# Thirteen early expert tiles in three fp32r products, their low parts summed by an adding DMA, and a gate loop written out

## The chip, the core and the metric

The kernel runs on one core of one Trainium2 chip. The metric is the device time of one execution in microseconds (us), the median of three runs. A core has five engines that run their own instruction streams: TensorE (PE, matrix products; PEld is its weight load), VectorE (DVE), ScalarE (ACT), GpSimd (POOL) and SyncE (SP), which here only starts transfers. Engines meet at semaphores. SBUF is the on-chip memory of the operands, PSUM that of the products.

## The reference, cut to what matters

Two layers. Each has a mixing part (chunked attention, retention, a state space model), and behind it the part that this case is about, a product-key expert mixer on 256 tokens of width 1024:

```python
q = (hf @ w_q).reshape(t, PEER_HEADS, 2, PEER_QDIM // 2)
s = jnp.einsum('thsd,hskd->thsk', q, subkeys)
top_s, top_i = lax.top_k(s, PEER_TOPK)                      # 16 of 128 keys, twice
cand_s = top_s[:, :, 0, :, None] + top_s[:, :, 1, None, :]
cand_i = top_i[:, :, 0, :, None] * PEER_NKEYS + top_i[:, :, 1, None, :]
best_s, best_pos = lax.top_k(cand_s.reshape(...), PEER_TOPK)
expert = jnp.take_along_axis(cand_i.reshape(...), best_pos, axis=-1)
gate = jax.nn.softmax(best_s, axis=-1)
ub = jnp.take(u_tab, eb, axis=0)
vb = jnp.take(v_tab, eb, axis=0)
act = jax.nn.gelu(jnp.einsum('thkd,td->thk', ub, hb))
return jnp.einsum('thk,thkd->td', (gb * act), vb)
```

All inputs and the output are float32.

## The kernel before

The kernel doesn't gather experts. It takes the 16384 experts as 128 tiles of 128, computes every expert's score for every token, multiplies by a gate that is zero where the expert wasn't picked, and sums the value rows. A float32 product is made in one of two ways: directly in fp32 (8 products of 128x128 by 128x256 for a tile, which the profile shows as 16 records), or in three fp32r products: the operands are split into a rounded high part and the low rest, and high by high, high by low and low by high are added (24 products of that size).

A layer's expert part has these stages.

- **Top-16 stage.** Sixteen query steps `n`: PE multiplies a tile of `w_q` (`query`, lines 798 to 802, three fp32r products), ScalarE copies the result (line 1177) and PE forms two key score blocks (`key_scores`, line 783); VectorE finds the top 16 of them and, two steps behind, of the candidate sums (`top16`, lines 1360 to 1367; `pairs`, line 1605). ScalarE makes the high part of each `w_q` tile (`w_q_high`, line 1044), GpSimd the low part (line 988). The `w_q` tiles come through four ring slots (`stream`, line 432); a slot's next load waits for the low part of its last tile. Then VectorE turns positions into keys (lines 1629 to 1655) and writes picks (line 1658), which PE transposes (line 834) and ScalarE copies (line 1194).
- **Ahead tiles.** PE is not filled by this, so it computes the scores of 20 of the 128 expert tiles early: `A_TOP` = 11 in the top-16 stage (`ahead`, line 795, in fp32, from raw tiles RAWU and the fp32 activations H32), four of them inside query steps 5, 8, 11 and 14 (`AHEAD_AT`), six behind the last key scores, one between the two sides of the picks; and `A_GATE` = 9 in the gate stage (`ahead_step`, line 863). SyncE issues the eleven loads of 512 KB together, behind the fourth query tile (line 485). Their gelus (line 1172) are stored to DRAM and fetched back in the expert loop.
- **Gate stage.** 64 groups of four tokens, in eight turns of eight. VectorE makes one-hots of the picks (lines 1671, 1673 and 1677), GpSimd the key one-hots of groups 0, 3 and 6 of a turn (line 998) after a small copy (line 994), ScalarE scales the gates into those of groups 1, 3, 5 and 7, PE multiplies them (line 855), and ScalarE copies the product (line 1207). The one-hots lie in four banks, so group c waits for the product of group c-4. VectorE's first turn is written out, the other seven are a hardware loop; PE and ScalarE have all eight written out; GpSimd's turns 2 to 7 are a loop.
- **Expert loop.** The other `NM` = 108 tiles. For each PE forms scores (lines 884 and 886) and, one tile behind, adds the value product (line 893, 12 products of 512 columns); ScalarE and VectorE split `u` and `v` and do gelu and gate. In layer 0 tiles 26 to 81 also carry work for the next layer's modulation (line 1743), and from tile 82 (`AHEAD_TILE`) on VectorE gates one ahead tile beside each loop tile (`gate_ahead`).
- **Tail.** The value products of the 20 ahead tiles, from nine buffers RAWV.

Each engine runs its own list in the order of the text; there is no planner. SBUF is laid out by hand, at offsets in floats from one base, and buffers of one stage lie over those of another.

## Time and profile before

| | us |
|---|---|
| median of 3 runs | 2105.37 |
| lowest and highest | 2104.90, 2107.96 |
| the profiled execution | 2113.12 |
| its span | 2111.3 |
| mean granted TensorE clock | 0.988 of full |

The profile shows one execution, and it was some 8 us longer than the runs without a profiler. Its page gives the busy share of each engine, the span in 40 slices, the chain of work that ended last, and the costliest groups of instructions; the trace can be asked for a stretch of time, an engine or a line. A row of the chain or the timeline starts with its start and its length in us and ends with the count of instructions that it merges; brackets hold the idle time before it and what ended that. Busy shares say little here: the stages have different limits.

### The profile page before, as it was taken

What the parts mean: (1) busy time and instruction counts of PE and PEld (TensorE: products, weight loads), DVE (VectorE), ACT (ScalarE), POOL (GpSimd) and SP (SyncE); (2) the same over time, 40 slices, a digit from 0 to 9 for tenths busy, and PEclk for the clock granted to TensorE, in tenths of its full rate; (3) what the DMA queues carried; (4) which work ended last, traced back from release to release, by engine and by line L of the source; (5) the groups of instructions that cost most, each with busy time, mean ns of one, the idle gap of its engine ahead of it and who ended that gap; (6) DMA issues with size and microseconds to landing.
All of it is one profiled execution on the core that took longest, in us unless ns stands there. A gap on an engine that the chain in (4) does not pass through costs nothing.

```text
span 2111.3 us, 33992 instructions
## 1 busy us (share of the span) xinstructions
PE 2023.7 (96%) x11188; PEld 1741.2 (82%) x11188; DVE 1583.3 (75%) x3436; ACT 974.9 (46%) x1619; POOL 266.0 (13%) x309
## 2 busy tenths in 40 slices
PE   5999999999999999999999989889999999999998
PEld 4798989888888888888778989788888888888876
DVE  8884999767888888887657268886767676768854
ACT  3223248655544444444522242675555555554443
POOL 2003339200000000000010041780000000000000
PEclk9999999999999999999999999999999999999999
DMA  9466311355778877555453462114555555555562
GB/s 372 141 264 263 111 54 60 128 188 199 272 282 306 294 276 281 188 179 195 158 179 100 138 232 80 56 53 165 186 190 187 207 210 203 185 184 180 180 237 69
DMA packets 115739, 392.19 MB, mean 186 GB/s; under 512 B 12752, under 2 KB 20816, under 8 KB 115152
## 3 DMA queue, kind: packets, MB, share of 16 engines
q1 hardware_dynamic: 115664, 391.21, 52.0%
q8 instruction: 44, 0.72, 0.1%
q14 instruction: 31, 0.25, 0.0%
HBM read 384.35 MB, written 6.82 MB: 185 GB/s over the span
## 4 chain that ended last, share of the span: by engine, by line
PE 68%; DVE 21%; issue 5%; ACT 2%; DMA 2%; DVEq 1%; SPq 0%; POOL 0%
PE ps L893 25%; PE ps L884 13%; PE ps L886 6%; PE ps L627 5%; DVE v_lo L1698 4%; PE ps L855 3%; PE ps L640 3%; DVE next_w_ada_ring L1743 3%; PE ps L769 2%; DVE u_lo L1693 2%; DVE onehot_gate L1677 2%; DVE gated L1706 1%; ACT gelu L1246 1%; PE ps L795 1%; PE ps L800 1%
## 5 line engine op out<-in xcount | busy, mean ns | idle before, releaser
L884 PE MATMUL ps<-h_hi_lo,u_hi 128*128 128x512 f32 x1728 | 630.5, 399 | 6.2 <-DVE u_lo L1693 5.8
L886 PE MATMUL ps<-h_hi_lo,u_lo 128*128 128x256 f32 x1512 | 425.3, 281 | 0.0
L884 PEld LDWEIGHTS ps<-h_hi_lo,u_hi 128*128 128x128 f32 x1728 | 326.0, 189 | 76.8 <-issue 6.5
L886 PEld LDWEIGHTS ps<-h_hi_lo,u_lo 128*128 128x128 f32 x1512 | 286.9, 190 | 8.1
L893 PE MATMUL ps<-v_hi,gated_hi 128*128 128x512 f32 x864 | 272.0, 396 | 5.4 <-DVE gated_lo L1712 4.3
L1693 DVE TENSOR_TENSOR u_lo<-weight_ring,u_hi 128x1024 fp32r<-128x1024 f32 x216 | 263.6, 1221 | 14.3 <-ACT u_hi L1235 11.1
L893 PE MATMUL ps<-v_lo,gated_hi 128*128 128x512 f32 x864 | 268.2, 392 | 0.0
L893 PE MATMUL ps<-v_hi,gated_lo 128*128 128x512 f32 x864 | 266.3, 389 | 0.0
L1698 DVE TENSOR_TENSOR v_lo<-weight_ring,v_hi 128x1024 fp32r<-128x1024 f32 x216 | 263.3, 1219 | 0.5 <-ACT v_hi L1240 0.5
L1240 ACT ACTIVATE v_hi<-weight_ring 128x1024 fp32r<-128x1024 f32 x216 | 227.4, 1053 | 53.6 <-PE ps L893 53.5
L1246 ACT ACTIVATE gelu<-gelu 128x256 f32<-128x256 f32 x216 | 90.3, 418 | 329.2 <-DVE gelu L1702 329.2
L1235 ACT ACTIVATE u_hi<-weight_ring 128x1024 fp32r<-128x1024 f32 x216 | 227.5, 1054 | 11.9 <-DMA weight_ring<-in_u_tab_dram 11.3
L1706 DVE TENSOR_TENSOR gated<-gelu,gates_T 128x256 f32<-128x256 f32 x216 | 92.0, 426 | 133.7 <-ACT gelu L1246 133.7
L893 PEld LDWEIGHTS ps<-v_lo,gated_hi 128*128 128x128 f32 x864 | 162.2, 188 | 36.2
L893 PEld LDWEIGHTS ps<-v_hi,gated_lo 128*128 128x128 f32 x864 | 162.2, 188 | 36.0
L893 PEld LDWEIGHTS ps<-v_hi,gated_hi 128*128 128x128 f32 x864 | 157.0, 188 | 41.5 <-issue 14.1
L1244 ACT ACTIVATE gelu<-ps 128x256 f32<-128x256 f32 x216 | 81.6, 378 | 221.1 <-PE ps L884 221.0
L998 POOL TENSOR_SCALAR onehot_key<-iota,key_columns 128x128 f32<-128x128 f32 x192 | 158.2, 838 | 2.3 <-PE ps L855 2.3
L855 PEld LDWEIGHTS ps<-onehot_gate,onehot_key 128*128 128x128 f32 x1024 | 132.6, 191 | 29.4 <-DVE onehot_gate L1673 11.4
L855 PE MATMUL ps<-onehot_gate,onehot_key 128*128 128x128 f32 x1024 | 136.6, 276 | 15.8 <-DVE onehot_gate L1673 8.8
L1710 DVE CAST gated_hi<-gated 128x256 fp32r<-128x256 f32 x216 | 63.5, 294 | 105.3 <-PE ps L893 100.2
L988 POOL TENSOR_TENSOR w_q_lo<-weight_ring,w_q_hi 128x1024 fp32r<-128x1024 f32 x32 | 76.0, 2381 | 335.7 <-ACT w_q_hi L1044 335.7
(314 smaller groups left out, 3115.4 us busy)
## 6 DMA issues: line engine op xcount, KB each, us to landing
weight_ring<-in_u_tab_dram SPq DMA_DIRECT2D x224, 512.0 KB, 4.5
weight_ring<-in_v_tab_dram SPq DMA_DIRECT2D x216, 512.0 KB, 3.5
next_w_ada_ring<-in_w_ada_dram SPq DMA_DIRECT2D x56, 512.0 KB, 4.4
weight_ring<-in_w_in_dram SPq DMA_DIRECT2D x46, 512.0 KB, 3.7
w_ada_ring<-in_w_ada_dram SPq DMA_DIRECT2D x40, 512.0 KB, 8.7
v_tail<-in_v_tab_dram SPq DMA_DIRECT2D x40, 512.0 KB, 4.7
weight_ring<-in_w_q_dram SPq DMA_DIRECT2D x32, 512.0 KB, 3.6
u_ahead<-in_u_tab_dram SPq DMA_DIRECT2D x22, 512.0 KB, 9.1
```

Source lines behind the costliest of these rows:

```text
L627: last = mm(PS[:, bank, 0:T], w[:, k, :], HT[:, k, :], start=(k == 0), stop=(k == KT - 1))
L855: last = mm(PS[:, c % 4, q * P:(q + 1) * P], OHB[:, c % 4, q, :], OHA[:, c % 4, q, :], start=True, stop=True)
L884: last = mm(both, UH[:, b, k, :], HB[:, :, k, :], start=(k == 0), stop=(k == KT - 1))
L886: mm(PS[:, 4 + b, 0:T], UL[:, b, k, :], HH[:, k, :], start=False, stop=False)
L893: last = mm(PS[:, 2 * t + d, :], g[:, t * P:(t + 1) * P], v[:, b, d * 512:(d + 1) * 512], start=start and n == 0, stop=stop and n == 2)
L998: last = nc.gpsimd.tensor_scalar(OHB[:, POOL_GROUPS[b] % 4, q, :], IOTA[:, 0:P], KEY4[:, b, q:q + 1], None, ALU.is_equal)
L1235: return fn(UH[:, b, :, :], RING[:, slot, :].rearrange("p (k n) -> p k n", n=P), ACT.Copy).then_inc(u_hi, 1)
L1240: return fn(VH[:, b, :], RING[:, slot, :], ACT.Copy).then_inc(v_hi, 1)
L1246: return fn(GE[:, b, :], GE[:, b, :], ACT.Gelu_apprx_tanh).then_inc(gelu_done, 1)
L1693: v.tensor_tensor(UL[:, b, :, :], RING[:, b, :].rearrange("p (k n) -> p k n", n=P), UH[:, b, :, :].bitcast(F32), ALU.subtract).then_inc(u_ ...
L1698: v.tensor_tensor(VL[:, b, :], RING[:, 2 + b, :], VH[:, b, :].bitcast(F32), ALU.subtract).then_inc(v_split, 1)
L1706: v.tensor_tensor(G32[:, :], GE[:, b, :], WT[:, i, :], ALU.mult).then_inc(g_prod, 1)
```

## The change

`A_TOP` goes from 11 to 13, so 22 tiles are ahead and 106 remain in the loop. The thirteen tiles are multiplied in three fp32r products. ScalarE writes the high part of a raw tile and its negated copy (`cut_ahead`); then a DMA issued by GpSimd reads the tile once more from DRAM and adds it into the negated copy, given to the DMA as a float32r tile; what stands there is the low part. Raw tiles have a ring of three buffers, high and low parts a ring of six pairs. Eight cuts stand in query steps (`CUT_AT`), five behind. The fp32 activations H32, still needed in the gate stage, are made later. The negated copy is written as float32r as well. The tail's nine buffers move to the start of the region. VectorE's loop over turns 1 to 7 of the gate stage becomes a Python loop, so its instructions are written out.

```diff
-A_TOP = 11
-A_RING = 11
+A_TOP = 13
+A_RING = 3
+CUT_AT = (1, 3, 5, 7, 9, 10, 12, 15)
-        V_AT = (0, 1024, 2048, 3072, 4096, 20480, 21504, 22528, 23552)
+        V_AT = range(0, 1024 * TAIL_RING, 1024)
+        AHEAD_PLACE = (0, 1, 2, 3, 0, 1, 2, 3, 4, 5, 0, 1, 2)
@@ SyncE
+                def ahead_raw(a):
+                    if a >= A_RING:
+                        sp.wait_ge(ahead_cut, l * A_TOP + a - A_RING + 1)
+                    sp.dma_start(RAWU[a % A_RING][:, :, :], u_tab[l, NM + a].rearrange("p (k n) -> p k n", n=P)).then_inc(
+                        in_ahead[a % A_RING], 16)
-                        for a in range(A_TOP):
-                            sp.dma_start(RAWU[a][:, :, :], u_tab[l, NM + a].rearrange("p (k n) -> p k n", n=P)).then_inc(in_ahead[a // 2], 16)
+                        for a in range(A_RING):
+                            ahead_raw(a)
+                    for a in range(A_RING, A_TOP):
+                        if a - A_RING < 7 and n == TILE_Q + min(15, CUT_AT[a - A_RING] + 4):
+                            ahead_raw(a)
+                ahead_raw(10)
@@ behind the first expert loads
                 ahead_late(1)
+                for a in range(11, A_TOP):
+                    ahead_raw(a)
@@ TensorE, ahead(a)
+                    pe.wait_ge(*ahead_summed(l, a))
                     for k in range(KT):
-                        last = mm(PS[:, 2 + a % 2, 0:T], RAWU[a][:, k, :], H32[:, k, :], start=(k == 0), stop=(k == KT - 1))
+                        mm(out, hi[:, k, :], HH[:, k, :], start=(k == 0), stop=False)
+                        mm(out, hi[:, k, :], HL[:, k, :], start=False, stop=False)
+                        last = mm(out, lo[:, k, :], HH[:, k, :], start=False, stop=(k == KT - 1))
@@ GpSimd
+                def add_raw(a):
+                    pool.wait_ge(ahead_cut, l * A_TOP + a + 1)
+                    place = AHEAD_PLACE[a]
+                    gp.dma_start(UAL[place][:, :, :], u_tab[l, NM + a].rearrange("p (k n) -> p k n", n=P),
+                                 accum_op=ALU.add).then_inc(ahead_low[place], 16)
+                    if n - 3 in CUT_AT:
+                        add_raw(CUT_AT.index(n - 3))
+                for a in range(7, A_TOP):
+                    add_raw(a)
@@ ScalarE
+                def cut_ahead(a):
+                    place = AHEAD_PLACE[a]
+                    act.wait_ge(*ahead_loaded(l, a))
+                    if place >= 4:
+                        act.wait_ge(q_mm, l * 16 + 20 - place)
+                    elif a >= 4:
+                        before = max(b for b in range(a) if AHEAD_PLACE[b] == place)
+                        act.wait_ge(ahead_mm, l * AHEAD + before + 1)
+                    fn(UAH[place][:, :, :], RAWU[a % A_RING][:, :, :], ACT.Copy)
+                    fn(UAL[place][:, :, :], RAWU[a % A_RING][:, :, :], ACT.Copy, scale=-1.0).then_inc(ahead_cut, 1)
+                    if n in CUT_AT:
+                        cut_ahead(CUT_AT.index(n))
-                gelu_ahead(4)
-                gelu_ahead(5)
+                for a in range(4, 9):
+                    gelu_ahead(a)
+                    cut_ahead(a + 4)
@@ VectorE, gate stage
-                with dve.Fori(1, 8) as i:
+                for i in range(1, 8):
                     for c in range(8):
                         dve.wait_ge(w_mm, i * 8 + (l * 64 + c - 3))
                         onehots(c, i * 32 + 4 * c)
@@ VectorE, expert loop
-                expert_tiles(AHEAD_TILE + AHEAD, NM - 2)
+                if AHEAD_TILE + AHEAD < NM - 2:
+                    expert_tiles(AHEAD_TILE + AHEAD, NM - 2)
```

## Rows read from the trace of the kernel before

**Rows 1.** The page: busy time by engine, and the chain by engine

```profile
PE 2023.7 (96%) x11188; PEld 1741.2 (82%) x11188; DVE 1583.3 (75%) x3436; ACT 974.9 (46%) x1619; POOL 266.0 (13%) x309
PE 68%; DVE 21%; issue 5%; ACT 2%; DMA 2%; DVEq 1%; SPq 0%; POOL 0%
```

**Rows 2.** The chain in order of time (start, us, what): value products, both layers

```profile
860.01 2.97 PE ps L893 x12
...
975.81 2.93 PE ps L893 x12
...
1001.96 58.43 PE ps L893 x252
...
1885.41 2.74 PE ps L893 x12
1890.96 2.75 PE ps L893 x12
2011.73 3.01 PE ps L893 x12
...
2037.96 57.88 PE ps L893 x252
```

**Rows 3.** The same chain, query steps of layer 1

```profile
1269.66 0.45 PE ps L783 x4
...
1272.98 0.45 PE ps L783 x4
...
1276.74 3.46 PE ps L795 x16
```

**Rows 4.** Groups by line, then timelines, chain and window, of the query steps

```profile
L800 PE MATMUL ps<-h_hi_lo,w_q_hi 128*128 128x256 f32 x128 | 39.1, 305 | 2.5 <-DVE h_hi_lo L1594 1.8 <-POOL w_q_lo L988 0.7
...
L1044 ACT ACTIVATE w_q_hi<-weight_ring 128x1024 fp32r<-128x1024 f32 x14 | 14.7, 1048 | 3.0 <-DMA weight_ring<-in_w_q_dram 3.0
...
L783 PE MATMUL ps<-subkeys_T,query_T 128*128 128x128 f32 x64 | 10.6, 290 | 3.3 <-DVE key_scores L1367 2.9 <-ACT query_T L1177 0.3
...
203.50 9.44 POOL L988 TENSOR_TENSOR w_q_lo<-weight_ring,w_q_hi 128x1024 fp32r<-128x1024 f32 x4 [2.74 <-ACT w_q_hi L1044]
...
204.02 8.94 DVE L1605 TENSOR_TENSOR candidates<-top_scores 128x32 f32<-128x32 f32 x4
...
216.43 4.51 PE ps L795 x16
...
1240.17 0.71 PE L783 MATMUL ps<-subkeys_T,query_T 128*128 128x128 f32 x4 [1.29 <-ACT query_T L1177]
1241.54 0.39 PE L800 MATMUL ps<-h_hi_lo,w_q_hi 128*128 128x256 f32 x1 [0.66 <-POOL w_q_lo L988]
...
1237.00:1247.00 10.00, 8.05 (x53) 7.66 (x52) 7.76 (x45) 6.69 (x13) 7.05 (x3) 0.83 0.58 215
```

**Rows 5.** The end of layer 0's top-16 stage: the chain, and PE's timeline

```profile
264.61 0.24 DVE best L1360
...
294.31 0.63 PE ps L834 x8
...
265.08 20.89 PE L795 MATMUL ps<-h_fp,u_ahead 128*128 128x256 f32 x96
```

**Rows 6.** Gate stage: windows (PE, PEld, DVE, ACT, POOL, clock, DMA), then timelines

```profile
311.20:322.39 11.19, 10.84 (x81) 10.10 (x81) 10.40 (x26) 9.45 (x26) 10.25 (x16) 1.00 0.18 59
...
1344.55:1357.11 12.56, 11.08 (x81) 10.03 (x81) 10.24 (x25) 9.48 (x26) 11.17 (x16) 1.00 0.15 52
...
1353.20 3.80 POOL L998 TENSOR_SCALAR onehot_key<-iota,key_columns 128x128 f32<-128x128 f32 x4
...
1357.15 2.54 POOL L998 TENSOR_SCALAR onehot_key<-iota,key_columns 128x128 f32<-128x128 f32 x4
...
1357.11 1.13 PE L855 MATMUL ps<-onehot_gate,onehot_key 128*128 128x128 f32 x8 [1.26 <-DVE onehot_gate L1673]
```

**Rows 7.** DMA issues of the page: KB each, median us from issue to landing

```profile
u_ahead<-in_u_tab_dram SPq DMA_DIRECT2D x22, 512.0 KB, 9.1
u_ahead_even<-in_u_tab_dram SPq DMA_DIRECT2D x10, 512.0 KB, 3.4
```

More of the change, by code:

```diff
@@ L183, in trunk @@
         CBN = at("next_cond", 4096, [P, D])
-        RAWU = [at(f"u_ahead_{a}", 2560 if a == 10 else 19200 + 1024 * a, [P, KT, P]) for a in range(A_TOP)]
+        RAWU = [at(f"u_ahead_{i}", o, [P, KT, P]) for i, o in enumerate((27392, 28416, 2560))]
+        UAH = [at(f"u_ahead_hi_{i}", o, [P, KT, P], F32R) for i, o in enumerate((19200, 21248, 23296, 25344, 38912, 40960))]
+        UAL = [at(f"u_ahead_lo_{i}", o, [P, KT, P], F32R) for i, o in enumerate((20224, 22272, 24320, 26368, 41984, 44032))]
         GEA = at("gelu_ahead", 29440, [P, A_TOP, T])
@@ L191, in trunk @@
         GER = at("gelu_back", 5120, [P, AHEAD, T])
[L192 to L194 removed]
+        GHA = at("gated_ahead_hi", 10752, [P, AHEAD, T], F32R)
+        GLA = at("gated_ahead_lo", 16384, [P, AHEAD, T], F32R)
+        V_AT = range(0, 1024 * TAIL_RING, 1024)
         RAWV = [at(f"v_tail_{a}", o, [P, D]) for a, o in enumerate(V_AT)]
@@ L339, in trunk @@
         s_sum = sem("expert_scores_summed")
-        in_ahead = [sem(f"u_ahead_pair_loaded_{a}") for a in range((A_RING + 1) // 2)]
+        in_ahead = [sem(f"u_ahead_loaded_{a}") for a in range(A_RING)]
+        ahead_cut = sem("u_ahead_hi_and_negated_done")
+        ahead_low = [sem(f"u_ahead_low_summed_{i}") for i in range(6)]
         in_late = [sem(f"u_ahead_late_loaded_{i}") for i in range(2)]
@@ L375, in trunk, with ahead_summed @@
         LATE_STORES = [len(range(i, A_GATE, 4)) for i in range(4)]
+        AHEAD_PLACE = (0, 1, 2, 3, 0, 1, 2, 3, 4, 5, 0, 1, 2)
         def ahead_loaded(l, a):
-            pair = a % A_RING // 2
-            tiles = [b // A_RING for b in range(A_TOP) if b % A_RING // 2 == pair]
-            return in_ahead[pair], 16 * (l * len(tiles) + sum(b <= a // A_RING for b in tiles))
+            return in_ahead[a % A_RING], 16 * (l * len(range(a % A_RING, A_TOP, A_RING)) + a // A_RING + 1)
+        def ahead_summed(l, a):
+            place = AHEAD_PLACE[a]
+            return ahead_low[place], 16 * (l * AHEAD_PLACE.count(place) + AHEAD_PLACE[:a + 1].count(place))
         TILE_IN, TILE_OUT, TILE_Q = 0, IN_TILES, IN_TILES + KT
@@ L788, in ahead @@
                 def ahead(a):
-                    pe.wait_ge(*ahead_loaded(l, a))
-                    if a == 0:
-                        pe.wait_ge(h32_done, l + 1)
+                    pe.wait_ge(*ahead_summed(l, a))
                     if a >= 2:
                         pe.wait_ge(ahead_gelu, l * AHEAD + a - 1)
+                    hi, lo, out = UAH[AHEAD_PLACE[a]], UAL[AHEAD_PLACE[a]], PS[:, 2 + a % 2, 0:T]
                     for k in range(KT):
-                        last = mm(PS[:, 2 + a % 2, 0:T], RAWU[a][:, k, :], H32[:, k, :], start=(k == 0), stop=(k == KT - 1))
+                        mm(out, hi[:, k, :], HH[:, k, :], start=(k == 0), stop=False)
+                        mm(out, hi[:, k, :], HL[:, k, :], start=False, stop=False)
+                        last = mm(out, lo[:, k, :], HH[:, k, :], start=False, stop=(k == KT - 1))
                     last.then_inc(ahead_mm, 1)
@@ L865, in ahead_step @@
                         last.then_inc(ahead_mm, 1)
+                pe.wait_ge(h32_done, l + 1)
                 for k in range(KT):
@@ L1169, in _ @@
                 w_q_high(l, 2)
+                def cut_ahead(a):
+                    place = AHEAD_PLACE[a]
+                    act.wait_ge(*ahead_loaded(l, a))
[6 more added lines that the diff above has]
+                    fn(UAL[place][:, :, :], RAWU[a % A_RING][:, :, :], ACT.Copy, scale=-1.0).then_inc(ahead_cut, 1)
                 def gelu_ahead(a):
@@ L1179, in _ @@
                         w_q_high(l, n + 3)
-                    if n < 4:
-                        for k in (2 * n, 2 * n + 1):
-                            last = fn(H32[:, k, :], HT[:, k, :], ACT.Identity, bias=MODS[l][:, SH2, k:k + 1])
-                        if n == 3:
-                            last.then_inc(h32_done, 1)
+                    if n in CUT_AT:
+                        cut_ahead(CUT_AT.index(n))
                     if n in AHEAD_AT:
                         gelu_ahead(AHEAD_AT.index(n))
-                gelu_ahead(4)
-                gelu_ahead(5)
+                for a in range(4, 9):
+                    gelu_ahead(a)
+                    cut_ahead(a + 4)
                 act.wait_ge(gate_in, l + 1)
                 fn(GATE[:, :, :], GATE[:, :, :], ACT.Exp).then_inc(gate_exp, 1)
-                for a in range(6, A_TOP):
+                for a in range(9, A_TOP):
                     gelu_ahead(a)
+                    if a < 11:
+                        for k in range(4 * (a - 9), 4 * (a - 9) + 4):
+                            last = fn(H32[:, k, :], HT[:, k, :], ACT.Identity, bias=MODS[l][:, SH2, k:k + 1])
+                        if a == 10:
+                            last.then_inc(h32_done, 1)
                 act.wait_ge(pickt_mm, l + 1)
```

2 lines of the change are left out of this document (removed).

## The prediction

> **What bounds the kernel now.** I read the page first: TensorE (PE) is busy 96% of the span and is 68% of the chain that ended last, VectorE (DVE) 21% [rows 1]. So PE's own work is the price of a tile, except where the chain leaves PE. The chain in order of time shows where. In the expert loop one tile costs 5.55 us on PE (start to start of the value products), 5.8 us where VectorE also gates the ahead tiles, and a tile of the tail only its value products: 58.43 us and 57.88 us for 21 of them [rows 2]. In the top-16 stage the query steps follow each other by 3.32 us, and an ahead tile adds 3.46 us [rows 3]: PE again, with a few holes that come from a late weight tile [rows 4]. From the last key scores (264.6 us in layer 0) to the gate products VectorE's chain of picks sets the time, some 29.7 us in which PE has room [rows 5]. In the gate stage a turn of eight groups takes 11.19 us in layer 0 and 12.56 us in layer 1, though the instructions are the same [rows 6].
>
> **Part 1, two tiles leave the loop.** There are 13+9 ahead tiles instead of 11+9, so the loop runs over 106 tiles, not 108. Gating of ahead tiles begins at tile 82 as before, and now covers 22 tiles: 82 to 103, with 2 plain tiles behind them instead of 6. Per layer 4 plain tiles go (4 x 5.55 = 22.2 us) and 2 gating tiles come (2 x 5.79 = 11.6 us in layer 0 by the step from 860.01 to 975.81 over 20 tiles; in layer 1, 120.77 us over 21 tiles, 5.75 each, 11.5 us): -10.6 and -10.7 us. The tail gets 2 tiles: 58.43/21 = 2.78 and 57.88/21 = 2.76 us each, +5.6 and +5.5 us. Net -5.0 and -5.2, together **-10.2 us**. Cover that shrinks: the tail's value tiles are fetched after the last ahead tile is gated, which was some seven tiles before the loop's end and is now two to three. From there PE still has about two score groups (2.8 us) and three value groups (2.75 us), some 14 us, and the same tiles land in 3.5 to 4.7 us [rows 7]: nothing, and a few us if four at once took over 10.
>
> **Part 2, the form of the ahead product.** Today 8 fp32 products (16 records) take 3.46 us. The query's form, 24 fp32r products of the same size, takes 3.32 - 0.45 = 2.87 us [rows 3]. Four ahead tiles stand inside the query steps, where PE is the chain: 4 x 0.59 = 2.36 us per layer, **-4.7 us**. Is VectorE late next? Its step there is 3.86 us, PE's would be (16 x 3.32 + 4 x 2.87)/16 = 4.04: it just keeps pace.
>
> **Part 3, the loads ahead of the query weights.** Eleven ahead loads are issued in one go before the fifth query tile, and ScalarE waits for that tile, 3.0 us in layer 0. PE waits behind it 0.3 + 0.7 us in layer 0 and 1.29 + 0.66 us in layer 1. Then in layer 0 GpSimd makes up four low parts without a pause (9.44 us), four tiny sums of VectorE take 8.94 us beside it, and PE waits 2.9 us for VectorE; the ahead tile after that wait takes 4.51 instead of 3.46 us. In layer 1 the granted clock from 1237 to 1247 us is 0.83, that is 1.2 GHz for 3.4 of 10 us, after PE's waits: 1.7 us lost [rows 4]. With 3 loads in front of it the tile comes some 10 us sooner and none of this need happen: -(1.0 + 2.9 + 1.05) = -4.95 and -(1.95 + 1.7) = -3.65, **-8.6 us**.
>
> The new waits: SyncE now waits for a cut at ScalarE before a reload, with the next query load queued behind it. A cut ends some 3.5 us into its step (query copy 0.38, query high part 1.05, two copies 2.1), and two transfers end 5 us later: 8.5 us. The tile is wanted by PE 4 x 3.32 = 13.3 us into the step, less 3.4 us for its high and low parts: 1.4 us spare, and 2.9 more where an ahead tile lies between, as it does for each of them. ScalarE waits up to 1.5 us there; query copies have 2.9 us of room. Nothing.
>
> **Part 4, the end of the top-16 stage.** Counted from the last key scores, PE today ends six ahead tiles at +21.2 us, and the first side's picks follow from there [rows 5]. Eight at 2.87 us end at +23.0. Then side 0 (2.1), the gates (0.4), the last ahead tile (2.9) and three quarters of side 1 (1.5) give +29.9, where VectorE has its last picks at +29.7; ScalarE's changed order (two table loads around the exponential, 1.28 us each, before the gelu of tile 9) costs 0.1. I put **+0.4 us per layer, +0.8**.
>
> **Part 5, the adding DMA.** The chain for tile a+4 is: tile a ends, gelu 0.4, two copies 2.1, adding DMA Z, product. PE comes round in 4 x 2.87 = 11.5 us, so Z may be 11.5 - 2.87 - 2.5 = 6.1 us. No row shows an adding DMA or any from GpSimd. Ends: 3.9 us, as a plain tile with its issue (3.4 to 3.6 landing, 0.43 issue), and 13 us or more if it queues as the eleven did (9.1 landing) and its extra read of the destination adds 3.5 [rows 7]. Nearest is the plain tile, with twice the traffic in SBUF: 7.5 us with issue. The ring of six then stalls PE by 1.4 us once in tiles 8 to 11, and tile 12 (start at 10.8 + 2Z = 25.8) not more. **+1.5 per layer, +3.0** (0 to 11 each). Inside the query steps tile 0 has about 8.7 us from its cut: covered. GpSimd's issues also hold VectorE's small sums, as in rows 4: 0 to 2.9 us per layer, I take 1: **+2.0**.
> The Trainium skill's page SBUF — State Buffer (SBUF: two separate sides) says that a DMA issued by GpSimd has its descriptors kept waiting while VectorE runs an operation on both ports. It speaks against this part; by it Z would be longest in VectorE's long arithmetic between +10 and +29. No row here has such a DMA. The page DMA: Bandwidth & Descriptors (Anatomy of one DMA — SWDGE path) gives 2.0 us plus bytes/436 GB/s, 3.2 us for a tile; an estimate by that would make the +3.0 zero.
>
> **Part 6, the gate loop written out.** The loop's turn costs VectorE gaps of 0.1 to 0.15 us. But VectorE then waits 0.68 us (layer 0) or 1.77 us (layer 1) for PE, and PE's first group of a turn starts 0.1 us after GpSimd's four key one-hots: 1353.20 + 3.80 = 1357.00, and PE at 1357.11. (The row puts the wait to VectorE, whose one-hots had ended by 1356.62; GpSimd ends last.) The same holds in layer 0, where PE starts 0.11 us after GpSimd too. So the turn is a ring of PE (3.97 us), GpSimd's copy and one-hots for the seventh group, and those for the next first; VectorE enters by slowing GpSimd: four one-hots cost 2.54 us with it idle, 3.25 to 3.33 in layer 0, 3.81 to 3.88 in layer 1 [rows 6]. Written out, the loop saves no time by its branch. It shifts VectorE by a tenth of a us against GpSimd, and the two layers part by no more than that. Bounds per turn: PE's own 8 x 1.325 = 10.6 us, and 12.56; seven turns a layer: from -(0.6 + 1.96) x 7 = -17.9 to +1.37 x 7 = +9.6 us. I take **0**.
> The Trainium skill's page Runtime: NRT & Kernel Launch (Instruction fetch mechanics) says that a taken branch breaks the sequential prefetch and can stall an engine. By it the unrolling would return at most the visible gaps, 0.24 x 14 = 3.4 us; the rows show them inside VectorE's waiting, so the sum takes none.
>
> **Sum**: -10.2 - 4.7 - 8.6 + 0.8 + 3.0 + 2.0 + 0 = **-17.7 us**. The profiled execution took 2113.1 us (span 2111.3), so it would take 2095.4; the median of the runs, 2105.4, is 7.7 below it and moves alike: **2087.7, say 2088 us**.
>
> **The rivals.**
> A, forecast: gate turns stay about as they are. 2088 (2081 to 2095). Chance 0.40.
> B, the gate turns get shorter: layer 1 falls into layer 0's pattern (-9.6 us: 2078) or both become bound by PE (2070). For it: same instructions, two speeds. Against: PE waits for GpSimd, not for the loop. 0.25.
> C, layer 0 falls into the 12.56 us pattern: +9.6, 2097. For it: VectorE without gaps takes the lead over GpSimd more often. 0.13. The same SBUF page's rule, one of the two engines holds the shared port for a whole instruction, is behind both B and C; the one-hots at 2.54 against 3.88 us agree that they hinder each other, though both run on in part.
> D, the added tiles come late: Z = 10 us. Tile 12 starts at 10.8 + 20 = 30.8 instead of 25.8; 5 us a layer in place of 1.9: 2094, with stalls inside the query steps 2100. 0.14.
> E, slower than before: the adding DMA itself becomes the bound. Each layer then pays 2Z - 15; with all other terms kept the gain of 17.7 + 3.8 = 21.5 us is gone at 10.8 us a layer, Z = 12.9 us. At Z = 15 the time is 2084 + 30 = 2114. For it: 9.1 us landings under load. 0.08.
>
> **How the numbers follow.** Below 2101.2 (0.2%, about what a measurement of this kernel can tell from no change) lie A, B, C and most of D: 0.87. Within 0.2%: the rest of D and a mild E, 0.06. Slower: 0.07. For 8 in 10 I leave out the far end of B and E: 2072 to 2101.
>
> **What would show it.** Right: the score rows of the loop fall from 216 to 212 tiles and the two tails take 63.9 and 63.4 us; ScalarE's wait for query weights nearly vanishes; ahead groups take 2.9 us; the turn of the gate stage, 11.2 and 12.6 us; GpSimd's one-hots tell which pattern. Wrong: adding DMAs landing over 9 us, PE waiting in front of ahead tiles 8 to 12, small sums of VectorE over 1 us each, or a tail whose high parts wait for their load.

## The result, and the profile after

The changed kernel takes 2116.5 us (median), 1.006 times the kernel before, 95% interval 1.0045 to 1.0074: 11 us slower by the medians and 13 by the ratio, where 17.7 us less were forecast. Three later executions, one each of e4 (3366 us), e11 (2199 us) and e12 (3215 us), fell into a slower state of the chip and are left out of all medians and ratios. Its profiled execution took 2121.41 us (span 2119.6). The page of the kernel after (busy time and the chain, as [rows 1]; the queues, whose columns are packets, MB and share of the 16 DMA engines' span; DMA issues, as [rows 7]):

```profile
PE 2018.2 (95%) x11396; PEld 1747.8 (82%) x11396; DVE 1575.3 (74%) x3428; ACT 1016.2 (48%) x1663; POOL 285.9 (13%) x335
q1 hardware_dynamic: 115952, 392.26, 52.5%
q0 software_dynamic: 3744, 13.63, 3.4%
PE 67%; DVE 18%; DMA 6%; issue 4%; ACT 3%; POOL 1%; DVEq 1%; SPq 0%; ACTq 0%
weight_ring<-in_w_q_dram SPq DMA_DIRECT2D x32, 512.0 KB, 5.7
u_ahead<-in_u_tab_dram SPq DMA_DIRECT2D x26, 512.0 KB, 4.5
u_ahead_lo<-in_u_tab_dram POOLq DMA_DIRECT2D x26, 512.0 KB, 9.1
```

TensorE's share of the chain hardly moved, VectorE's fell from 21% to 18%, and DMA, 2% of it before, is 6% now; the last line, the adding DMAs' landing, is new. The chain in order of time names the places in layer 0's top-16 stage:

```profile
269.86 17.63 DMA u_ahead<-in_u_tab_dram
287.54 0.94 issue
288.48 1.05 ACT u_ahead_lo L1216
```

The plain load of ahead tile 11 takes 17.6 us. ScalarE's and VectorE's timelines beside it (start, us, engine, line, operation; in brackets the idle time before it and what ended it):

```profile
279.72 0.38 ACT L1220 ACTIVATE gelu_ahead<-ps 128x256 f32<-128x256 f32 x1 [4.13 <-PE ps L818]
287.51 1.06 ACT L1215 ACTIVATE u_ahead_hi<-u_ahead 128x1024 fp32r<-128x1024 f32 x1 [7.41 <-DMA u_ahead<-in_u_tab_dram]
...
292.99 0.42 ACT L1236 ACTIVATE gates<-gates 128x256 f32<-128x256 f32 x1
```

```profile
281.68 5.45 DVE L1709 SCALAR_TENSOR_TENSOR picked_keys<-pos_a_f,top_keys_f 128x256 bf16<-128x256 f32 x16
293.43 0.42 DVE L1703 TENSOR_REDUCE gate_sum<-gates 128x16 f32<-128x256 f32 x1 [6.30 <-ACT gates L1236]
...
306.19 0.94 DVE L1728 TENSOR_SCALAR onehot_gate<-iota,picks_T 128x128 f32<-128x128 f32 x3 [6.15 <-ACT picks_T L1245]
```

ScalarE stands 7.4 us for tile 11; the gates' exponential is queued behind its parts; VectorE waits 6.3 us for that and 6.2 us for the transposed picks. In [rows 5] VectorE's chain of picks ran through, but for 1.6 us before the first one-hot made from the transposed picks. Windows of the two parts of layer 0's top-16 stage, from the first h_T to VectorE's positions ("past") and from there to the first one-hot; of before, then of after (busy us of PE, PEld, DVE, ACT, POOL, then granted clock, DMA share, GB/s):

```profile
186.92:275.63 88.71, 82.96 (x561) 78.81 (x562) 80.66 (x469) 31.60 (x56) 33.30 (x14) 0.94 0.44 158
275.63:295.81 20.18, 19.04 (x135) 16.58 (x135) 18.11 (x54) 3.91 (x7) 0.00 (x0) 1.00 0.18 72
```

```profile
190.17:275.03 84.86, 77.08 (x616) 76.11 (x616) 75.42 (x469) 47.03 (x68) 42.00 (x24) 0.96 0.71 198
275.03:306.19 31.16, 25.96 (x215) 25.20 (x216) 18.19 (x54) 13.51 (x23) 2.59 (x3) 0.89 0.76 216
```

The first part gave back 3.9 us; the second costs 11.0 us more for the same 18.1 us of VectorE, with the DMA engines' share at 0.76 instead of 0.18. In layer 1 the parts are 87.8 and 33.9 us (before: 86.3 and 20.2). In all seventeen traces the second part is 18.6 to 18.7 us plus VectorE's two waits, for the exponential and for the transposed picks: 6.3 + 6.2 us in layer 0 of after, 5.9 + 9.2 in layer 1, 0 + 1.6 in both layers before. The loop and the tails did what was forecast: 276 value products in one go, 63.89 us in layer 0.

### The profile page after: what moved, and what is told of

It reads as the page before. It is cut to its first block, busy times and chain, and to the rows that moved or that the text cites. A ratio compares the mean times of both kernels' runs of the same rounds, so it can differ in the third digit from the quotient of the medians.

```text
span 2119.6 us, 33931 instructions
## 1 busy us (share of the span) xinstructions
PE 2018.2 (95%) x11396; PEld 1747.8 (82%) x11396; DVE 1575.3 (74%) x3428; ACT 1016.2 (48%) x1663; POOL 285.9 (13%) x335
## 3 DMA queue, kind: packets, MB, share of 16 engines
q1 hardware_dynamic: 115952, 392.26, 52.5%
## 4 chain that ended last, share of the span: by engine, by line
PE 67%; DVE 18%; DMA 6%; issue 4%; ACT 3%; POOL 1%; DVEq 1%; SPq 0%; ACTq 0%
PE ps L918 25%; PE ps L909 12%; PE ps L911 6%; PE ps L649 5%; PE ps L879 4%; DVE v_lo L1749 4%; PE ps L662 3%; DMA weight_ring<-in_w_q_dram 3%; PE ps L791 3%; DVE next_w_ada_ring L1794 3%; DVE u_lo L1744 2%; PE ps L887 2%; DMA u_ahead<-in_u_tab_dram 2%; DVE gated L1757 1%; ACT gelu L1297 1%
## 5 line engine op out<-in xcount | busy, mean ns | idle before, releaser
L909 PE MATMUL ps<-h_hi_lo,u_hi 128*128 128x512 f32 x1696 | 617.6, 398 | 6.2 <-DVE u_lo L1744 5.8
L911 PE MATMUL ps<-h_hi_lo,u_lo 128*128 128x256 f32 x1484 | 417.5, 281 | 0.0
L909 PEld LDWEIGHTS ps<-h_hi_lo,u_hi 128*128 128x128 f32 x1696 | 319.6, 189 | 74.9 <-issue 6.5
L911 PEld LDWEIGHTS ps<-h_hi_lo,u_lo 128*128 128x128 f32 x1484 | 281.3, 190 | 8.0
L918 PE MATMUL ps<-v_hi,gated_hi 128*128 128x512 f32 x848 | 267.6, 397 | 5.1 <-DVE gated_lo L1763 3.9
L1744 DVE TENSOR_TENSOR u_lo<-weight_ring,u_hi 128x1024 fp32r<-128x1024 f32 x212 | 258.7, 1221 | 14.6 <-ACT u_hi L1286 11.3
L918 PE MATMUL ps<-v_lo,gated_hi 128*128 128x512 f32 x848 | 263.5, 392 | 0.0
L918 PE MATMUL ps<-v_hi,gated_lo 128*128 128x512 f32 x848 | 261.7, 390 | 0.0
L1749 DVE TENSOR_TENSOR v_lo<-weight_ring,v_hi 128x1024 fp32r<-128x1024 f32 x212 | 258.3, 1218 | 0.0
L1297 ACT ACTIVATE gelu<-gelu 128x256 f32<-128x256 f32 x212 | 88.6, 418 | 333.7 <-DVE gelu L1753 333.7
L1291 ACT ACTIVATE v_hi<-weight_ring 128x1024 fp32r<-128x1024 f32 x212 | 223.1, 1053 | 51.1 <-PE ps L918 51.1
L879 PEld LDWEIGHTS ps<-onehot_gate,onehot_key 128*128 128x128 f32 x1024 | 133.1, 192 | 23.6 <-DVE onehot_gate L1724 9.1
```

Source lines behind the costliest of these rows:

```text
L879: last = mm(PS[:, c % 4, q * P:(q + 1) * P], OHB[:, c % 4, q, :], OHA[:, c % 4, q, :], start=True, stop=True)
L909: last = mm(both, UH[:, b, k, :], HB[:, :, k, :], start=(k == 0), stop=(k == KT - 1))
L911: mm(PS[:, 4 + b, 0:T], UL[:, b, k, :], HH[:, k, :], start=False, stop=False)
L918: last = mm(PS[:, 2 * t + d, :], g[:, t * P:(t + 1) * P], v[:, b, d * 512:(d + 1) * 512], start=start and n == 0, stop=stop and n == 2)
L1291: return fn(VH[:, b, :], RING[:, slot, :], ACT.Copy).then_inc(v_hi, 1)
L1297: return fn(GE[:, b, :], GE[:, b, :], ACT.Gelu_apprx_tanh).then_inc(gelu_done, 1)
```

## The experiments

All kernels in one table. The ratio goes against the kernel before on the same chip (whose median moved between 2103.7 and 2108.2 us from one set of runs to the next, so small differences are read from ratios). The last columns are, for each layer, h_T to positions + positions to first one-hot, from the starts of those instructions in each trace.

| kernel | us | ratio, 95% | layer 0 | layer 1 |
|---|---|---|---|---|
| before | 2105.4 | 1 | 88.7 + 20.2 | 86.3 + 20.2 |
| b_again (before, one execution) | 2108.2 | | 90.6 + 20.2 | 86.3 + 21.5 |
| after | 2116.5 | 1.006 (1.0045-1.0074) | 84.9 + 31.2 | 87.8 + 33.9 |
| e1_unroll_alone | 2108.1 | 1.001 (0.9997-1.0024) | 88.6 + 20.2 | 88.6 + 20.2 |
| e2_loop_back | 2115.9 | 1.0043 (1.0027-1.006) | 86.9 + 31.5 | 87.8 + 31.1 |
| e3_raws_first | 2110.2 | 1.0018 (1.0008-1.0027) | 88.6 + 26.8 | 87.6 + 26.2 |
| e4_query_first | 2115.3 | 1.0044 (1.0028-1.0059) | 85.2 + 30.8 | 87.9 + 30.0 |
| e5_both_orders | 2107.7 | 1.0012 (0.9997-1.0026) | 85.1 + 28.3 | 87.8 + 24.3 |
| e6_early_cuts | 2103.3 | 0.9988 (0.9975-1.0002) | 85.5 + 25.3 | 86.8 + 23.1 |
| e7_plain_second | 2095.2 | 0.9952 (0.9934-0.9969) | 82.6 + 22.7 | 83.9 + 24.8 |
| e8_no_adding | 2085.5 | 0.9906 (0.988-0.9933) | 82.7 + 20.2 | 81.4 + 20.2 |
| e9_subtract | 2138.1 | 1.0145 (1.0122-1.0169) | 108.1 + 20.3 | 105.4 + 20.2 |
| e10_none_at_end | 2098.3 | 0.9959 (0.9944-0.9974) | 85.1 + 20.6 | 86.2 + 20.6 |
| e11_mixed | 2111.3 | 1.0032 (1.0019-1.0044) | 94.6 + 20.3 | 93.7 + 20.9 |
| e12_half_added | 2091.5 | 0.9939 (0.9917-0.9961) | 80.7 + 24.3 | 81.2 + 25.9 |
| e13_fp32_at_end | 2092.4 | 0.9929 (0.9913-0.9945) | 82.1 + 23.6 | 83.4 + 22.1 |
| e14_all_fp32 | 2097.7 | 0.995 (0.9936-0.9963) | 84.4 + 23.8 | 84.4 + 23.8 |

The last two columns come from one execution each, and they scatter: before and b_again are the same kernel and differ by 1.9 us to the positions of layer 0 and 1.4 us at the end of layer 1; after and e2 run the same instructions up to layer 0's one-hots and differ by 2.1 us to its positions, and, with no difference but the gate loop, by 2.8 us at the end of layer 1. So a difference of 2 to 3 us in one of these columns shows little by itself.

**The gate loop.** Before with `for i in range(1, 8)`, after with `dve.Fori(1, 8)`, and before once more for its trace:

> The kernel before with VectorE's gate loop written out and nothing else. Theory (the loop's turn, not the new top-16 stage, took 7.2 us out of layer 1's gate stage, 112.8 to 105.6 us): 2098 us, ratio 0.9966, layer 1's gate stage near 106 us, layer 0's still near 104. Rival (layer 1's gate stage changed because of something else in the new kernel, as the start of its one-hots against GpSimd): 2105 us, layer 1 still at 112 to 113 us.

> The changed kernel with VectorE's gate loop as a loop again. Theory: layer 1's gate stage goes back from 105.6 to about 112.8 us, layer 0's stays near 104: 2116.5 + 7 = 2123.5 us. Rival (the writing out did nothing, the shorter stage comes from elsewhere): 2116.5 us, layer 1 at 106 us.

> The kernel before, once more, for its trace. Theory (the 9 us of layer 1's gate stage, 110.4 against 101.3 us in layer 0, are how that one execution fell, since neither writing the loop out nor looping it again in the changed kernel showed them): layer 1's gate stage at 101 to 104 us and a span near 2103 us. Rival (they belong to the kernel with the loop and the old top-16 stage): 110 us again in layer 1.

The theory fell. Written out alone, the loop brings nothing (0 to 0.2% slower); put back, it costs nothing (2115.9 against 2116.5). The stage (first one-hot to VectorE's first sum of the expert loop) takes 101.3 and 110.4 us in the profiled execution of before, but 99.7 and 100.9 in b_again, 101.5 and 101.6 in e1, 101.2 and 101.1 in e2. The slow turns of [rows 6] were how that one execution fell. They account for its 2113.1 us against a median of 2105.4, and for this: the profiled executions understate what the change costs: 8 us between them, 13 by the ratio.

**The order on SyncE's queue.** For tile 11, and for the query weights:

```
-                ahead_raw(10)
+                for a in range(10, A_TOP):
+                    ahead_raw(a)
                 for v in (0, 1):
...
                 ahead_late(1)
-                for a in range(11, A_TOP):
-                    ahead_raw(a)
```

> The changed kernel with the plain loads of ahead tiles 11 and 12 issued right after that of tile 10, ahead of the three expert loads and the first late load. Theory (tile 11's load takes 17.6 us because four other tiles stand in front of it, and ScalarE, then the gates' exponential and VectorE's picks wait behind it): ScalarE's wait for the plain tile falls from 7.4 and 8.1 us to 0 to 2 us, VectorE's for the exponential from 6 us to under 2, and each layer's top-16 stage is 5 to 7 us shorter: 2105 us. Rival (the adding DMAs of tiles 8 to 12 are what is slow, the loads in front are no matter): tile 11's product is late by its adding DMA anyway, 0 to 2 us a layer, 2113 to 2116 us.

```
-                        if a - A_RING < 7 and n == TILE_Q + min(15, CUT_AT[a - A_RING] + 4):
+                        if a - A_RING < 7 and n == TILE_Q + min(15, CUT_AT[a - A_RING] + 6):
```

> The changed kernel with each plain reload inside the query steps issued two query loads later (4 becomes 6 in the offset from the cut's step), so that SyncE waits for the cut only when the query loads of the next two steps are out. Theory (order on SyncE's queue: the query load stands behind SyncE's wait for a cut): ScalarE's waits for query weights fall from 19.0 us in layer 0's stage and from 38.2 us in layer 1 to near before's 3 us, and the two stages get some 12 us shorter together: 2104 us. Rival (bandwidth: adding DMAs slow every query load in flight, whatever the order): landings of query loads stay at 5 to 6 us, waits fall by less than half, 2112 to 2116 us.

> The changed kernel with both re-orderings of SyncE's queue (plain tiles 11 and 12 ahead of the expert loads; plain reloads two query loads later). Theory after the first runs (VectorE is the bound from the first scores to its picks, so the missing query weights cost only what VectorE waits; the end of the stage costs by tile 11's late load): the gains add, 6 us from the first and 1 to 3 from the second: 2108 to 2110 us, from the stage's start to the positions about 85 us, from there to the one-hots 26 to 27 us. Rival (the two compete for the same DMA engines: an earlier reload makes the adding DMAs late): no better than the first alone, 2110 to 2112 us.

The first holds in its mechanism: ScalarE's wait for the plain tile falls from 7.4 to 0.8 us, VectorE's for the exponential is gone, and the end of the stage is 4.3 and 7.6 us shorter. It brings about half of what was expected, 2110.2 us instead of 2105. What is left at the end of layer 0 (26.8 us against 20.2) is this wait (engine, tile, line, releaser: us in total, times, longest):

```profile
DVE onehot_gate L1727 <- ACT picks_T L1244: 8.2, 1, 8.2
```

It was 1.6 us before. TensorE makes these picks behind the late ahead tiles. The second experiment shows where I had misread the stage. ScalarE's wait for query weights in layer 0 of after (19.0 us; 18.5 in layer 1, where my expectation had put 38.2):

```profile
ACT w_q_hi L1080 <- DMA weight_ring<-in_w_q_dram: 19.0, 8, 5.9
```

In e4 it vanishes from ScalarE's list in both layers, yet the positions come after 85.2 and 87.9 us, as in after: 2115.3. 19 us of ScalarE's waiting there cost nearly nothing.

What does count is VectorE. Its time to the positions is, in all seventeen traces, a constant of 59.2 to 59.6 us, plus its waits for scores, plus its 64 small sums of candidates:

| kernel, layer | to positions | small sums | waits for scores | rest |
|---|---|---|---|---|
| before, 0 | 88.7 | 22.3 | 5.7 + 1.2 | 59.5 |
| after, 1 | 87.8 | 15.6 | 4.6 + 8.3 | 59.3 |
| e4, 0 | 85.2 | 20.9 | 4.5 + 0.4 | 59.4 |
| e8, 0 | 82.7 | 17.4 | 5.7 | 59.6 |
| e14, 0 | 84.4 | 19.2 | 5.8 | 59.4 |
| e9, 0 | 108.1 | 42.8 | 5.7 | 59.6 |

VectorE's waits in that window of layer 1 of after (engine, tile, line, releaser: us in total, times, longest):

```profile
DVE best L1411 <- PE ps L805: 8.3, 6, 2.5
DVE top_scores L1411 <- PE ps L805: 4.6, 2, 3.7
```

e4 trades one for the other: in layer 1 the waits fall by 7.2 us and the sums grow from 15.6 to 22.7. The traces show where the sums grow: in all seventeen, a sum that lies beside none of GpSimd's subtractions takes at most 0.20 us. In layer 1 of after 13 of the 64 sums lie beside a subtraction and take 8.4 us, in e4 it is 15 sums and 15.7 us. That VectorE's waiting is what moves the sums away from the subtractions is likely, and was not tested by itself.

e5 has both orders and takes 2107.7 us, close to its theory (2108 to 2110); the intervals of e3 and e5 overlap.

**The adding DMA itself.** First, on top of e5, ScalarE's parts for tiles 8 to 12 one ahead tile earlier:

```
+                cut_ahead(8)
                 for a in range(4, 9):
                     gelu_ahead(a)
-                    cut_ahead(a + 4)
+                    if a < 8:
+                        cut_ahead(a + 5)
```

> As the kernel with both re-orderings, and ScalarE makes the high and negated parts of tiles 8 to 12 one ahead tile earlier (tile 8's before the gelu of tile 4, tile 9's before that of tile 5, and so on). Theory (what is left of the end of the stage, 26.5 us against before's 20.2, is mostly TensorE waiting for adding DMAs that take 8 to 12 us where 6.1 fit): one ahead tile more of slack, 2.9 us, takes most of the 4.2 us of waits, and the end of the stage is 23 to 24 us: 2 to 3 us less a layer, 2103 to 2105 us. Rival (the adding DMAs share bandwidth: issued earlier they land as late): end of the stage stays at 26 us, 2108 us.

Then, each by itself in the changed kernel: a plain copy instead of the addition, no second load, none for tiles 7 to 12, and the addition for half of each tile.

```
-                    gp.dma_start(UAL[place][:, :, :], u_tab[l, NM + a].rearrange("p (k n) -> p k n", n=P),
-                                 accum_op=ALU.add).then_inc(ahead_low[place], 16)
+                    gp.dma_start(UAL[place][:, :, :], u_tab[l, NM + a].rearrange("p (k n) -> p k n", n=P)
+                                 ).then_inc(ahead_low[place], 16)
```

> The changed kernel with GpSimd's second load as a plain copy, without the addition; the low parts are then the whole tiles, so the ahead tiles of the output are computed from other weights. Theory (adding itself is dear: it reads and writes the destination): landings fall from 9.1 to about 5 us and TensorE's waits for them vanish, the rest of the queueing stays; 2112 us. Rival (the length comes from 512 KB more beside the other loads and from GpSimd's queue, not from the addition): landings stay over 8 us and the time at 2116 us.

```
-                    pe.wait_ge(*ahead_summed(l, a))
+                    pe.wait_ge(ahead_cut, l * A_TOP + a + 1)
...
-                    if n - 3 in CUT_AT:
-                        add_raw(CUT_AT.index(n - 3))
-                for a in range(7, A_TOP):
-                    add_raw(a)
```

> The changed kernel without the 26 adding DMAs; TensorE waits for the cut alone. It leaves the addition out, so low parts are minus the high parts. Theory (second loads crowd the DMA engines and hold up plain tile 11, and GpSimd's issues and TensorE's waits come on top): query loads land in under 4.5 us, tile 11's plain load in under 10, TensorE's and ScalarE's waits at the end of the stage nearly vanish, end of the stage 22 us: 2116.5 - 2 x 9 = 2098 us. Rival (the end of the stage is long because of the order on SyncE's queue and of ScalarE's exponential behind the last cuts, with or without the additions): 2108 us or more.

For e10 only the additions of tiles 7 to 12 go (the last two of these lines), and TensorE waits for the cut alone from tile 7 on.

> The changed kernel without the adding DMAs of tiles 7 to 12 (TensorE waits for their cut alone; their low parts are minus the high parts), those of tiles 0 to 6 kept. Theory from the stage times (the additions cost 11 to 13.6 us a layer after the query steps and 2.2 to 6.3 us in them): the end of the stage falls to 20 to 22 us, the time from the start to the positions stays at 85 to 88 us: 2116.5 - 2 x 11 = 2094 us. Rival (what the seven inside the query steps delay is carried through the end): 2100 us or more.

```
-                    gp.dma_start(UAL[place][:, :, :], u_tab[l, NM + a].rearrange("p (k n) -> p k n", n=P),
+                    gp.dma_start(UAL[place][:, 0:KT // 2, :], u_tab[l, NM + a].rearrange("p (k n) -> p k n", n=P)[:, 0:KT // 2, :],
                                  accum_op=ALU.add).then_inc(ahead_low[place], 16)
```

> The changed kernel with adding DMAs over the first half of each tile only, 256 KB in place of 512; it leaves the addition out for the other half. Theory (what costs is the time of the shared DMA engines: 3.4% of 16 engines' span for 26 adding DMAs, 2.8 us each, against 1.8%, 1.4 us each, as plain copies): the cost of 31 us over the kernel without them is about halved, landings fall from 9.1 to 5 or 6 us, 2099 to 2102 us. Rival (what costs is fixed per DMA, GpSimd's issue, the descriptors and the latency, whatever the size): landings stay over 8 us, 2110 us or more.

Without the second load the kernel takes 2085.5 us: **the additions cost 31 us** (32 by the ratios). As plain copies they cost 9.7, over half a tile 5.9 (10 and 7 by the ratios; e8's own interval is 5.6 us wide to either side, so these two are not told apart, but both are far from 31). The queue's line of the page, of e7 and then of e12:

```profile
q0 software_dynamic: 3744, 13.63, 1.8%
```

```profile
q0 software_dynamic: 3744, 6.82, 1.9%
```

In us of all 16 engines for one of the 26: 3.4% of 2119.6 / 26 = 2.8 us with the addition, 1.8% of 2094.1 / 26 = 1.45 us as a copy, 1.9% of 2089.7 / 26 = 1.5 us for an added half. A plain load by SyncE takes 52.5% of 2119.6 / 392.26 MB x 0.524 MB = 1.5 us. So adding doubles the engines' time, and the price follows that time, though not in proportion: none 0, half 6 to 10, all of it 31 us. The instructions that issue the second loads, with shortest, median and longest ns of the issue, and under each the time from issue to landing; of after, e7 and e12:

```profile
L1013 POOL DMA_DIRECT2D u_ahead_lo<-in_u_tab_dram x26: 849/862/1017, 206.3 to 1331.2; - x26
DMA to landing us min/median/max: 5.6/9.1/12.4
```

```profile
L1013 POOL DMA_DIRECT2D u_ahead_lo<-in_u_tab_dram x26: 530/570/743, 202.7 to 1308.7; - x26
DMA to landing us min/median/max: 4.5/6.7/10.3
```

```profile
L1013 POOL DMA_DIRECT2D u_ahead_lo<-in_u_tab_dram x26: 847/864/1022, 201.3 to 1303.0; - x26
DMA to landing us min/median/max: 4.1/7.5/9.1
```

e12 issues as slowly as after and moves as many packets, and it costs 6 us: the issue on GpSimd and the number of packets are not the price. Latency alone does not order the kernels either: e12's loads land later than e7's in the median and it is no slower. Both the engines' time and the landing are worse in after, and the two were not varied apart. My theory for e8 (2098) was 12 us too high, that for e7 (2112) took too little for the addition, and that for e12 (half the price, 2099 to 2102) too much for the half. The two windows of layer 0 in e8, to set against those of after:

```profile
189.40:272.10 82.70, 79.94 (x646) 79.61 (x647) 75.86 (x469) 48.36 (x70) 33.56 (x14) 0.95 0.48 179
272.10:292.28 20.18, 19.24 (x188) 18.54 (x187) 18.11 (x54) 12.41 (x21) 0.00 (x0) 1.00 0.24 98
```

The DMA share is 0.48 and 0.24 instead of 0.71 and 0.76, and the end of the stage is 20.2 us again. What the addition does to others shows in the landings (shortest, median, longest us, of the plain ahead loads of after, then of e8):

```profile
DMA to landing us min/median/max: 3.6/4.5/17.6
```

```profile
DMA to landing us min/median/max: 3.4/3.7/6.1
```

Tile 11's load stands behind the same four tiles in e8 and needs at most 6.1 us (and no plain ahead load of e7 more than 9.0). The order on SyncE's queue was thus only the place where the additions struck. e10 takes 18.2 of the 31 us off (21 by the ratios), between its theory (2094) and its rival (2100 or more): the end of the stage is 20.6 us in both layers, and the time to the positions stays. The seven additions a layer in the query steps carry the rest. In the traces of after and e8 the difference lies in VectorE's waits: for scores 2.7 and 8.4 us more in after (layers 0 and 1), for the exponential 6.3 and 5.9, for the transposed picks 4.6 and 7.7. Its sums are 0.3 and 1.8 us shorter. e6's cuts save 4.4 us, as expected: with more slack, some of the additions' time is hidden, and TensorE still waits 4.1 us in four times in layer 0.

**Another way to the low part.** GpSimd subtracts, as for the query weights; then only for tiles 7 to 12 (both with the orders and cuts of e6):

```
-                    gp.dma_start(UAL[place][:, :, :], u_tab[l, NM + a]..., accum_op=ALU.add).then_inc(ahead_low[place], 16)
+                    gp.tensor_tensor(UAL[place][:, :, :], RAWU[a % A_RING][:, :, :],
+                                     UAH[place][:, :, :].bitcast(F32), ALU.subtract).then_inc(ahead_low[0], 1)
```

> The kernel with both re-orderings and the earlier cuts, and GpSimd makes the low parts by subtraction from the tile that is already in SBUF (as it does for the query weights, 2.35 us each) in place of the 26 adding DMAs; ScalarE's negated copies go, a plain reload waits for the subtraction. Theory (what the change loses is the second, adding load of each tile: 31 us between the changed kernel and the one without it): end of the stage back to 20 to 21 us; VectorE's small sums run longer beside 13 more subtractions, 2 to 4 us a layer: 2090 to 2094 us, some 12 us under before. Rival (GpSimd's arithmetic holds VectorE, which is the bound of the stage, as much as the DMAs did): to the positions 88 to 90 us instead of 82.7, 2100 us or more.

> The kernel with both re-orderings and the earlier cuts, with adding DMAs for tiles 0 to 6 and GpSimd's subtraction for tiles 7 to 12, most of which fall behind the query steps. Theory (adding DMAs are dear at the end of the stage, 14 us in two layers by the kernel without them there; subtractions are dear only beside VectorE's small sums of the query steps, 1.8 us each there by the kernel that subtracts everywhere): to the positions 85 to 88 us, end of the stage 20 to 22 us, 2096 to 2099 us, some 8 us under before. Rival (VectorE's last picks and positions up to +10 us after the last scores are held as the small sums are): two to four us more a layer, 2101 to 2106 us.

Both theories fell, the first badly: 2138.1 us. Groups of VectorE to the positions in layer 0, of e9 and then of e8 (busy us, mean ns of one):

```profile
L1656 DVE TENSOR_TENSOR candidates<-top_scores 128x16 f32<-128x16 f32 x32 | 19.7, 656 | 0.0
L1656 DVE TENSOR_TENSOR candidates<-top_scores 128x32 f32<-128x32 f32 x16 | 14.0, 877 | 0.5
L1656 DVE TENSOR_TENSOR candidates<-top_scores 128x8 f32<-128x8 f32 x16 | 9.1, 569 | 0.0
```

```profile
L1652 DVE TENSOR_TENSOR candidates<-top_scores 128x32 f32<-128x32 f32 x16 | 8.7, 542 | 0.5
L1652 DVE TENSOR_TENSOR candidates<-top_scores 128x8 f32<-128x8 f32 x16 | 4.7, 296 | 0.0
L1652 DVE TENSOR_TENSOR candidates<-top_scores 128x16 f32<-128x16 f32 x32 | 4.0, 165 | 0.0
```

Thirteen subtractions more make the sums 25.4 us longer, 2.0 us for each of 2.4 us. The end of the stage is 20.3 us, so the ahead tiles no longer delay it. In e11 the six subtractions begin at 262.5 us, when VectorE still sorts the last scores, and its sums take 28.8 us where they take 20.9 in e6: 94.6 us to the positions. The Trainium skill's page SBUF — State Buffer (SBUF: two separate sides) has the two engines share one pair of ports, held for a whole instruction where VectorE reads two operands from SBUF and GpSimd reads SBUF too. The sums here agree (2.0 us for each subtraction of 2.4), and at this place that rule was worth more than anything in my sum.

**A version that beats both.** Tiles 0 to 6 keep three products and their addition; 7 to 12 are plain fp32 products from the loaded tile, as before. Then (e14) all thirteen so, in eleven buffers, with tiles 11 and 12 loaded into the first two again:

```
+                        if a >= 7:
+                            last = mm(out, ahead_at(a)[:, k, :], H32[:, k, :], start=(k == 0), stop=(k == KT - 1))
+                            continue
                         mm(out, hi[:, k, :], HH[:, k, :], start=(k == 0), stop=False)
...
-                for a in range(7, A_TOP):
-                    add_raw(a)
```

> Thirteen ahead tiles with the orders of the kernel with both re-orderings, where tiles 0 to 6 keep the three products and their adding DMA, and tiles 7 to 12 are plain fp32 products from the loaded tile as in the kernel before: no cut, no second load, and the fp32 copy of the hidden state made in the first query steps again. Theory (additions are dear where several stand in a row behind the last scores, 14 us in two layers; fp32 products cost 0.6 us more each, of which TensorE has some to spare before the picks): the end of the stage 22 to 23 us instead of 31, to the positions 86 us, 2099 to 2102 us, under before's 2105 by 0.2 to 0.3%. Rival (six products of 3.46 us put TensorE in front of the picks: 3 x 2.9 + 6 x 3.5 + 3.6 = 33 us from the last scores where VectorE needs 29.7): end of the stage 24 us or more, 2104 us.

```
-                        if a >= 7:
+                        if a >= 0:
...
-                    elif a >= A_RING:
-                        sp.wait_ge(ahead_cut, l * 7 + a - A_RING + 1)
+                    if a >= 11:
+                        sp.wait_ge(ahead_mm, l * AHEAD + a - 10)
...
+                        if a < 11 and n == TILE_Q + a + 1:
+                            ahead_raw(a)
```

> Thirteen ahead tiles, all as plain fp32 products in the form of the kernel before: eleven buffers, tile 11 and 12 loaded again into the first two, no cut, no adding DMA; three loads ahead of the fifth query tile and the others one for each query step. Theory (VectorE bounds the stage up to its picks, so TensorE's 0.6 us less a tile is worth nothing inside the query steps, and the three products with their second loads are pure cost): as fast as the kernel with fp32 products at the end, 2090 to 2094 us. Rival (the cheaper form does carry part of the gain in the query steps, as the prediction had it, 4.7 us in four tiles of two layers): 2096 to 2100 us.

e13 takes 2092.4 us, 0.7% under before and 1.3% under the changed kernel, and is better than its theory: to the positions 82.1 and 83.4 us. e14 goes to the rival: 2097.7 us. Both have the two tiles fewer in the loop and the spread loads. What parts them is the cheaper form of tiles 0 to 6 together with its seven additions a layer, and the steps at which the plain loads are issued. It is worth 0.2% or 4.4 us by the ratios, whose intervals overlap a little: 2.3 and 1.0 us to the positions, 0.2 and 1.7 us at the end, each within the scatter of one trace. What the form alone is worth was not isolated.

## Why the prediction was wrong, step by step

- **Part 1** (-10.2): held. From the end of layer 0's gate stage to layer 1's h_T, and from the end of layer 1's gate stage to the end: 819.2 and 667.8 us after, against 824.0 to 827.3 and 672.7 to 674.3 in the traces of before, b_again and e1, 10 to 15 us less together.
- **Parts 2 and 3** (-4.7 and -8.6): near in size, wrong in mechanism. e8, the change without its second loads, reaches the positions 6.0 and 4.8 us sooner than before, 10.8 of the 13.3. e14, with spread loads and the old form, does so 4.3 and 1.9 us sooner; e13 adds the 2.3 and 1.0 above. But I counted them as TensorE's time on the chain. VectorE's own waits and sums carry them. The 3.86 us that I took as VectorE's step is its step when nothing disturbs it; from the first to the last step of layer 0 of before the mean is 4.7 us, with the waits and with the sums beside subtractions. So VectorE was not the engine that just kept pace. That the size came out near is luck in part.
- **"The new waits ... Nothing"** in part 3: right for the waits of ScalarE (e4), by luck. Two transfers do not end 5 us later beside an addition; the query loads' median is 5.7 us, and ScalarE waited 19 us where I allowed 1.5.
- **Part 4** (+0.8): nothing of it came, 20.2 us in both layers of e8 against 20.2.
- **Part 5** (+5.0) is the step that failed: **it measured 31 us**. I took Z = 7.5 us from "the plain tile, with twice the traffic in SBUF"; issue to landing was 9.1 us in the median and up to 12.4. By my own sum that gives no more than rival D, 2094 us. The sum lacked a term: I costed the addition as a latency in its own chain, and put the time that it takes from the shared DMA engines at nothing, without a reason. It takes 2.8 us of all 16 engines, in a stretch where expert loads, late loads and plain reloads stand too (such loads land in 3.4 us when alone and in 9.1 us in a crowd [rows 7]), so tile 11's plain load took 17.6 us. The second thing overlooked is what stands behind that load in ScalarE's order: the exponential, and with it VectorE's picks. Rival E had the sign and nearly the size (2114 us), with a chance of 0.08, though its 2Z - 15 is not the mechanism: Z never came to 12.9 us in the median of after. The estimate from the Trainium skill's page DMA: Bandwidth & Descriptors (Anatomy of one DMA — SWDGE path), 3.2 us, was too low even for the plain copy, 4.5 us at the least and 6.7 in the median.
- GpSimd's issues (+2.0): not seen. VectorE's small sums take 17.1 and 15.6 us in after, with the 26 issues of 0.86 us, and 17.4 in both layers of e8 without them. What the Trainium skill's page SBUF — State Buffer (SBUF: two separate sides) says of descriptors kept waiting while VectorE works on both ports was not told apart from the crowd on the engines.
- **Part 6** (0): held for the writing out (e1, e2). Rivals B and C had no ground: the pattern comes and goes with the execution, and I should have asked why the profiled one lay 7.7 us over the median.

Parts 1 to 4 make -22.7 us, 2082.7; e8 measured 2085.5.

What stays open: how VectorE's waits, in which the 31 us show, go back to TensorE's waits for additions, to other loads made late, and to the clock, which was 0.89 at the end of layer 0's stage after and 1.00 in e8. e13's positions come sooner than e10's, which also has seven additions: in layer 0 by shorter sums (12.4 us against 17.3), in layer 1 by shorter waits for scores (6.2 against 11.4); why they fall so stays open too.

## What to carry to other kernels

Cost a DMA that is added by the time it takes from the shared engines, not only by its own latency: look at the DMA share of the stretch, at what else is in flight there, and at what stands behind each of those loads in every in-order queue. And before counting an engine's shorter work as a gain, write the stage's time as the sum of the bounding engine's own rows (here: constant, sums, waits); a wait that is not among them, even one of 19 us, may be worth nothing.

## What the runs showed of the hardware

- An adding DMA of 512 KB took 2.8 us of all 16 engines against 1.45 to 1.5 us for a copy, 0.86 us to issue on GpSimd against 0.57, and 5.6 us at best to land, 9.1 us in the median.
- In this kernel the price of the 26 second loads rose faster than the engines' time: 6 to 10 us for half of it, 31 us for all.
- A GpSimd subtraction of 2.4 us lengthened VectorE's small fp32 sums (means of 165 to 542 ns in e8) by 2.0 us, nearly its whole length. A sum beside no subtraction took at most 0.20 us, in all traces.
- Two executions of the same kernel differed by 9.5 us in one layer's gate stage, 110.4 against 100.9.
